# Gate building with one 256-column fp32r product a token, its high half copied by ScalarE and its low half added by VectorE

## The reference, cut to what matters

```python
s1, i1 = lax.top_k(s[:, :, 0], PEER_TOPK)
s2, i2 = lax.top_k(s[:, :, 1], PEER_TOPK)
cand = (s1[..., :, None] + s2[..., None, :]).reshape(PEER_BLOCK, PEER_HEADS, PEER_TOPK * PEER_TOPK)
sc, ic = lax.top_k(cand, PEER_TOPK)
e1 = jnp.take_along_axis(i1, ic // PEER_TOPK, axis=-1)
e2 = jnp.take_along_axis(i2, ic % PEER_TOPK, axis=-1)
idx = e1 * PEER_NKEYS + e2
gate = jax.nn.softmax(sc, axis=-1)
act = jax.nn.gelu(jnp.einsum('td,thkd->thk', xb, u[idx]).astype(jnp.float32), approximate=False)
return jnp.einsum('thk,thkd->td', (gate * act).astype(xb.dtype), v[idx])
```

## Time and profile before

| | us |
|---|---|
| median of 3 runs | 4364.64 |
| lowest and highest run | 4364.55, 4371.59 |
| the profiled execution, its own time | 4372.93 |
| the span of its trace | 4370.9 |
| mean granted TensorE clock | 0.973 |

### The profile page before, as it was taken

How to read it: one execution, slowest core, us unless ns; L and a number is a source line. 1 busy time by engine, 2 the same in 40 slices (tenths; PEclk the granted TensorE clock), 3 DMA queues, 4 the chain that set the end, 5 groups by cost and what they waited for, 6 DMA issues and landing times. The chain is left out here.

```text
span 4370.9 us, 85782 instructions
## 1 busy us (share of the span) xinstructions
PE 4123.5 (94%) x32794; PEld 3775.2 (86%) x32794; DVE 3159.1 (72%) x5937; ACT 1417.5 (32%) x2207; POOL 1317.5 (30%) x1006
## 2 busy tenths in 40 slices
PE   8999999997669979999999998999999999999998
PEld 5898888886548869787878887999999999999998
DVE  5621334444852368889976665999999999999998
ACT  4212222112552222233356774222222222222224
POOL 4333330000022200244532333444434444443441
PEclk9999999999879999999999999999999999999999
DMA  6665665564643211244435447999999999999995
GB/s 220 215 205 179 227 233 180 188 247 126 174 143 105 111 54 40 76 144 135 144 118 200 178 174 268 312 297 303 302 299 302 300 301 298 301 303 299 299 303 194
DMA packets 527665, 928.68 MB, mean 212 GB/s; under 512 B 286400, under 2 KB 353728, under 8 KB 523344
## 3 DMA queue, kind: packets, MB, share of 16 engines
q1 hardware_dynamic: 391584, 549.91, 38.5%
q0 software_dynamic: 81056, 346.96, 23.5%
q10 hardware_dynamic: 54816, 28.85, 2.3%
HBM read 786.05 MB, written 206.30 MB: 227 GB/s over the span
## 5 line engine op out<-in xcount | busy, mean ns | idle before, releaser
L3513 POOL DMA_INDIRECT ex_rows<-expert_rows,ex_here x512 | 586.7, 1146 | 953.6 <-DVE acc_tok L3734 863.8
L3734 DVE SCALAR_TENSOR_TENSOR acc_tok<-ex_rows,ex_wsp,acc_tok 128x1024 f32<-128x1024 f32 x512 | 634.5, 1281 | 0.0
L2837 PE MATMUL ex_psa<-x_dense_high,eg_u_high 128*128 128x288 f32 x2048 | 604.5, 295 | 13.4 <-ACT ex_w L3625 10.3
L2837 PE MATMUL ex_psa<-x_dense_low,eg_u_high 128*128 128x288 f32 x2048 | 604.6, 295 | 0.0
L2837 PE MATMUL ex_psa<-x_dense_high,eg_u_low 128*128 128x288 f32 x2048 | 604.2, 295 | 0.0
L2928 POOL TENSOR_TENSOR eg_u_low<-eg_u,eg_u_high 128x1024 fp32r<-128x1024 f32 x130 | 340.8, 2622 | 797.4 <-ACT eg_u_high L2923 797.4
L3545 PE MATMUL ex_pso<-ex_w_high,ex_v_high 128*128 128x288 f32 x2048 | 442.2, 298 | 7.6 <-DVE acc L3716 7.6
L3625 ACT ACTIVATE ex_w<-ex_psa 128x288 f32<-128x288 f32 x256 | 105.4, 412 | 1055.3 <-PE ex_psa L2837 1055.3
L3545 PE MATMUL ex_pso<-ex_w_high,ex_v_low 128*128 128x288 f32 x2048 | 440.7, 297 | 0.0
L3545 PE MATMUL ex_pso<-ex_w_low,ex_v_high 128*128 128x288 f32 x2048 | 439.3, 296 | 0.0
L3716 DVE TENSOR_TENSOR acc<-ex_pso,acc 128x576 f32<-128x576 f32 x512 | 374.7, 753 | 45.1 <-PE ex_pso L3545 45.1
(11 more groups left out here) (537 smaller groups left out, 9042.1 us busy)
## 6 DMA issues: line engine op xcount, KB each, us to landing
eg_u<-in_u SPq DMA_DIRECT2D x256, 512.0 KB, 5.1
expert_rows<-in_v SPq DMA_DIRECT2D x128, 512.0 KB, 7.2
ex_v<-in_v SPq DMA_DIRECT2D x128, 512.0 KB, 6.2
weights<-wt_stage SPq DMA_DIRECT2D x9, 4096.0 KB, 12.9
ex_g<-weights SPq DMA_DIRECT2D x128, 288.0 KB, 6.8
expert_rows<-eg_act SPq DMA_DIRECT2D x256, 128.0 KB, 1.7
proj<-in_out POOLq DMA_DIRECT2D x50, 548.5 KB, 6.3
in_w<-in_w_in SPq DMA_DIRECT2D x50, 512.0 KB, 5.1
```

The source lines that it names most:

```text
L2837: yield nc.tensor.matmul(out[:, 0:b - a], w[:, kc, :], half[:, kc, a:b], start=n == 0, stop=n == len(passes) - 1)
L3513: pool.indirect_dma_start(rows[i][:, :], None, table, index(here[par][:, t, j:j + 1]), element_offset=ROW_RUNS[t][0]).then_inc(s_row[i], 16)
L3734: v.scalar_tensor_tensor(out=acc_tok[:, t, :], in0=rows[i][:, at:at + D], scalar=wsp[:, i:i + 1], in1=acc_tok[:, t, :], op0=ALU.mult, op1= ...
```

## The change

BATCH becomes 4, so there are 16 batches in a block (144 in all), RING is 8 slots, FILL is 9, and FINISHED is worked out from FILL (after batches 2, 5, 7, 10, 13 and 15 of a block).

The gate is split once at the start into a high part, rounded to fp32r, and a low part (selT gets a fourth slice): ACT rounds, DVE subtracts, for the first 64 tokens and then for the others. one1 gets two matrices a token, side by side: the one-hot times the low part of the gate, and the one-hot times the high part. one2 stays a bare one-hot. Both are fp32r, and a token is one product with 256 columns, into 1 KB of PSUM: low gates, then high gates.

The one1 pair is made for the first 2 tokens of a batch by a DVE comparison into the high place and two ACT multiplications, and for the other 2 by one DVE scalar_tensor_tensor each (gated). ACT copies the high half of a batch from PSUM to stage (copy_high, 512 elements) and DVE adds the low half from PSUM to it in place (add_low, 512 elements). DVE does this for batch m - 2 within batch m, between gated and one2, and waits there for ACT's copy. ACT's order is: the copy for batch n, the gates for batch n + 2, then gelu and high where one is due. The iota gets a buffer of its own. SP's and POOL's programs stay as they are; the wait of SP for a block's last evacuation now ends with DVE's last addition.

The diff, cut to its core:

```diff
--- before.py
+++ after.py
@@ -2821,7 +2821,7 @@
-BATCH = 8
+BATCH = 4
...
@@ -3178,24 +3178,30 @@
     BANKS = 2
     SG_ = SPREAD_GROUPS
     FILL = SG_ * 3 * KC // NB
+    NHOT = NTB * NB
     HALF = BATCH // 2
+    LOW, HIGH = 2, 3
     with ExitStack() as ctx:
         sb = lambda n, s, dt=F32: ctx.enter_context(nc.sbuf_tensor(f"wt_{n}", s, dt))
         iota = sb("iota", [P, NK])
-        one1 = sb("one1", [P, RING, NK])
-        one2 = sb("one2", [P, RING, NK])
-        iota_i = one2[:, 0, :].bitcast(I32)
+        one1 = sb("one1", [P, RING, 2, NK], F32R)
+        one2 = sb("one2", [P, RING, NK], F32R)
+        iota_i = sb("iota_i", [P, NK], I32)[:, :]
         stages = sb("stage", [P, 2, NK, TB])
         stage = [stages[:, 1], stages[:, 0]]
-        ps = ctx.enter_context(nc.psum_tensor("wt_ps", [P, BANKS, BATCH, NK], F32))
+        ps = ctx.enter_context(nc.psum_tensor("wt_ps", [P, BANKS, BATCH, 2, NK], F32))
         early.banks(ctx, "wte")
         EACH, ERING = 2 * SG_, early.RING
         assert EACH % ERING == 0
         s_io = k.sem("wt_iota_step")
+        s_high = k.sem("wt_gates_rounded")
+        s_low = k.sem("wt_gates_split")
         s_st = k.s_weights_stored = [k.sem(f"wt_stored{i}") for i in range(2)]
 
         batches = [f"batch{n}" for n in range(NB)]
-        OH = Progress(k.sem("wt_onehots"), *batches)
+        hots = [f"hot{n}" for n in range(NB)]
+        CP = Progress(k.sem("wt_high_copied"), *batches)
+        OH = Progress(k.sem("wt_onehots"), *[s for pair in zip(hots, batches) for s in pair])
         GA = Progress(k.sem("wt_gated"), *batches)
         PE = Progress(k.sem("wt_matmul"), *batches)
         EV = Progress(k.sem("wt_evac"), *batches)
@@ -3220,9 +3226,8 @@
         late = TOPK_EARLY - 1 + early.RING
         late_group = (late, late % ERING, late // ERING)
 
-        def slots(n, lo=0, hi=BATCH):
-            at = n * BATCH % RING
-            return slice(at + lo, at + hi)
+        def ring(m):
+            return m * BATCH % RING
...
@@ -3258,26 +3263,47 @@
             def _(dve):
                 v = nc.vector
                 OH.credit(dve)
+
+                def split(n, lo, hi):
+                    dve.wait_ge(s_high, n)
+                    w = selT[:, LOW, lo:hi]
+                    v.tensor_tensor(w, w, selT[:, HIGH, lo:hi], ALU.subtract).then_inc(s_low, 1)
+
+                def onehots(out, side, lo, hi):
+                    return v.tensor_tensor(out, bc(iota[:, :].unsqueeze(1), [P, hi - lo, NK]),
+                                           bc(selT[:, side, lo:hi].unsqueeze(2), [P, hi - lo, NK]), ALU.is_equal)
+
+                def gated(out, c):
+                    v.scalar_tensor_tensor(out=out, in0=bc(iota[:, :].unsqueeze(1), [P, 2, NK]), scalar=selT[:, 0, c:c + 1],
+                                           in1=bc(selT[:, LOW:HIGH + 1, c:c + 1], [P, 2, NK]),
+                                           op0=ALU.is_equal, op1=ALU.mult)
+
+                def add_low(m):
+                    b, n = divmod(m, NB)
+                    dve.wait_ge(CP.sem, CP.now(batches[n], b))
+                    out = stage[b % 2][:, :, n * BATCH:(n + 1) * BATCH]
+                    v.tensor_tensor(out, out, ps[:, m % BANKS, :, 0, :].rearrange("p t f -> p f t"),
+                                    ALU.add).then_inc(*EV.inc(batches[n]))
+
+                split(1, 0, TB)
+                dve.wait_ge(s_low, 1)
                 dve.wait_ge(s_io, 2)
-
-                def body(b, slot, r):
-                    for n in range(NB):
-                        dve.wait_ge(PE.sem, PE.back(n, AHEAD, b))
-                        t0 = n * BATCH
-                        col = TB * b + t0
-
-                        def onehots(out, side, lo, hi):
-                            cnt = hi - lo
-                            return v.tensor_tensor(out[:, slots(n, lo, hi), :], bc(iota[:, :].unsqueeze(1), [P, cnt, NK]),
-                                                   bc(selT[:, side, col + lo:col + hi].unsqueeze(2), [P, cnt, NK]),
-                                                   ALU.is_equal)
-                        onehots(one1, 0, 0, BATCH)
-                        onehots(one2, 1, 0, HALF)
-                        for t in range(t0 + HALF, t0 + BATCH):
-                            last = v.tensor_scalar(one2[:, t % RING, :], iota[:, :], selT[:, 1, TB * b + t:TB * b + t + 1],
-                                                   selT[:, 2, TB * b + t:TB * b + t + 1], ALU.is_equal, ALU.mult)
-                        last.then_inc(*OH.inc(batches[n]))
-                in_line(body)
+                for m in range(NHOT):
+                    b, n = divmod(m, NB)
+                    if m == AHEAD:
+                        split(2, TB, TD)
+                    if m == NB:
+                        dve.wait_ge(s_low, 2)
+                    at, col = ring(m), BATCH * m
+                    dve.wait_ge(PE.sem, PE.back(n, AHEAD, b))
+                    onehots(one1[:, at:at + HALF, 1, :], 0, col, col + HALF).then_inc(*OH.inc(hots[n]))
+                    for t in range(HALF, BATCH):
+                        gated(one1[:, at + t, :, :], col + t)
+                    if m >= AHEAD:
+                        add_low(m - AHEAD)
+                    onehots(one2[:, at:at + BATCH, :], 1, col, col + BATCH).then_inc(*OH.inc(batches[n]))
+                for m in range(NHOT - AHEAD, NHOT):
+                    add_low(m)
 
             @block.tensor
             def _(pe):
@@ -3292,8 +3318,8 @@
                         pe.wait_ge(OH.sem, OH.now(batches[n], b))
                         pe.wait_ge(GA.sem, GA.now(batches[n], b))
                         pe.wait_ge(EV.sem, EV.back(n, BANKS, b))
-                        for t in range(n * BATCH, (n + 1) * BATCH):
-                            mm = nc.tensor.matmul(ps[:, n % BANKS, t % BATCH, :], one2[:, t % RING, :], one1[:, t % RING, :],
+                        for t in range(BATCH):
+                            mm = nc.tensor.matmul(ps[:, n % BANKS, t, :, :], one2[:, ring(n) + t, :], one1[:, ring(n) + t, :, :],
                                                   start=True, stop=True)
                         mm.then_inc(*PE.inc(batches[n]))
                         if b:
@@ -3306,39 +3332,45 @@
             @block.scalar
             def _(act):
                 GA.credit(act)
+                CP.credit(act)
                 EV.credit(act)
                 for i in range(2):
                     act.sem_inc(s_st[i], 16)
-                FINISHED = {2: 0, 3: 1, 4: 2, 6: 3, 7: 4}
-
-                def gate(b, n):
-                    act.wait_ge(OH.sem, OH.now(batches[n], b))
-                    for t in range(n * BATCH, n * BATCH + HALF):
-                        o_ = one2[:, t % RING, :]
-                        last = nc.scalar.activation(o_, o_, ACT.Copy, scale=selT[:, 2, TB * b + t:TB * b + t + 1])
+                FINISHED = {-(-3 * KC * (i + 1) // FILL) - 1: i for i in range(SG_)}
+
+                def rounded(lo, hi):
+                    nc.scalar.activation(selT[:, HIGH, lo:hi].bitcast(F32R), selT[:, LOW, lo:hi], ACT.Copy).then_inc(s_high, 1)
+
+                def gate(m):
+                    b, n = divmod(m, NB)
+                    act.wait_ge(OH.sem, OH.now(hots[n], b))
+                    for t in range(HALF):
+                        hot, c = one1[:, ring(m) + t, :, :], BATCH * m + t
+                        nc.scalar.activation(hot[:, 0, :], hot[:, 1, :], ACT.Copy, scale=selT[:, LOW, c:c + 1])
+                        last = nc.scalar.activation(hot[:, 1, :], hot[:, 1, :], ACT.Copy, scale=selT[:, HIGH, c:c + 1])
                     last.then_inc(*GA.inc(batches[n]))
 
+                def copy_high(b, slot, r, n):
+                    if n == 0:
+                        act.wait_ge(s_st[slot], 16 * r + 16)
+                    act.wait_ge(PE.sem, PE.now(batches[n], b))
+                    nc.scalar.activation(stage[slot][:, :, n * BATCH:(n + 1) * BATCH],
+                                         ps[:, n % BANKS, :, 1, :].rearrange("p t f -> p f t"),
+                                         ACT.Copy).then_inc(*CP.inc(batches[n]))
+
                 def body(b, slot, r):
-                    def evac(n):
-                        if n == 0:
-                            act.wait_ge(s_st[slot], 16 * r + 16)
-                        act.wait_ge(PE.sem, PE.now(batches[n], b))
-                        dst = stage[slot][:, :, n * BATCH:(n + 1) * BATCH].rearrange("p f t -> p t f")
-                        nc.scalar.activation(dst, ps[:, n % BANKS, :, :], ACT.Copy).then_inc(*EV.inc(batches[n]))
-
                     for n in range(NB):
-                        if n:
-                            gate(b, n)
-                            evac(n - 1)
+                        copy_high(b, slot, r, n)
+                        if NB * b + n + AHEAD < NHOT:
+                            gate(NB * b + n + AHEAD)
                         if n in FINISHED:
```

(15 more changed lines are left out.)

## The result

The changed kernel takes 4413.65 us (median of 4 runs, 4406.89 to 4417.9) against 4368.11 (4 runs, 4364.55 to 4374.26): a ratio of 1.0103, 95% interval 1.0090 to 1.0117, slower by 45.5 us. The prediction was 4413.0, range 4335 to 4465, slower with a chance of 0.64. One more run of the kernel before stands beside the three known at the prediction, and lifts its median from 4364.64 to 4368.11.

A forecast was written before the change was run, and what follows sets the result against it. PE bounds the kernel before, DVE after: 333 us of DVE steps, 95 of stalls, 56 of u waits, 1 and 5.5 make a 490.5 us stage against 442.1, +48, so 4413 us, range 4335 to 4465.

The forecast's parts named there:

- The bound: In the phase_spread stage, PE bounds the kernel before (DVE waits 162.6 us for it); after the change DVE does.
- PE's part: PE's products in the stage: 2.51 us per new batch, giving back 61 us, a 381 us stage if PE stayed the bound.
- DVE's part: DVE's steps in each of 144 new batches: 2.31 us a batch, 333 us in all.
- Rival 4: DVE's low addition reads PSUM in 1 KB steps, taking 1.01 us instead of 0.60: 37 us more, 4450 us; chance 0.14.
- The stalls: DVE instructions with two SBUF operands stand while POOL makes u low halves: 1.76 us for each of 54 operations, 95 us.
- The u waits: At 8 block ends ACT waits 7.0 us for the u tile queued behind the weights, with nothing covering it: 56 us.
- The sum: Stage total: 333 + 95 + 56 + 1 + 5.5 = 490.5 us against 442.1, +48, forecasting 4413 us.
- small edits: Roundings and splits of the gates on ACT and DVE: 1 us; iota buffer and selT slice cost nothing.
- The clock: PE's lower clock level after standing idle in the stage: no cost, at most 8 us.

The follow-up runs named there:

- e3: Changed kernel with the u load issued before the 4 MB weights store and POOL making one eighth of the stage's u low halves: 4309.90 us, ratio 0.9871.
- e4: Kernel before the change, with SP issuing a block's first u load ahead of the previous block's weights store: 4358.75 us, ratio 0.9981.
- e1: Changed kernel with SP issuing a block's first u load ahead of the previous block's 4 MB weights store: 4355.65 us, ratio 0.9974.
- e10: e1's kernel with DVE's addition of the low half moved behind one2: 4350.28 us, ratio 0.9966.
- e5: Kernel before the change, with POOL making only one eighth of each u tile's low half in the stage: 4370.01 us, ratio 0.9998.
- e2: Changed kernel with POOL making only one eighth of each u tile's low half in the stage: 4367.41 us, ratio 0.9998.
- e8: e1's kernel with ACT multiplying gates into three tokens and DVE into one in every second batch: 4371.06 us, ratio 1.0001.
- e9: e7b's kernel with ACT multiplying gates into three tokens and DVE into one in every second batch: 4368.57 us, ratio 0.9996.
- e7b: e1's kernel with DVE instead of POOL making the u low half in the stage: 4345.13 us, ratio 0.9940.
- e11: e7b's kernel with DVE's addition of the low half moved behind one2: 4333.20 us, ratio 0.9926.

## Why the prediction was right, step by step

**The bound.** It turned from PE to DVE, as predicted: 162.6 us of DVE waiting for PE became 6.5.

**PE's part.** Forecast 2.51 us a batch and a stage of 381; e3 showed 2.57 in the batch above (2.54 in the median of its batches) and 382.1. The four new products take 0.47 us, 0.12 each. Where nothing else holds the stage it is 442.1 - 382.1 = 60.0 us shorter, close to the forecast 61. Not all of that is the new product's: e3 also has the load order, which gave the kernel before 8.6 us (e4). Against e4's 433.5 the change gives back 51.4.

**DVE's part.** Forecast 2.31 us a batch; an undisturbed one runs from comparison to comparison in 2.33 (in e1's timeline from 2389.50 to 2391.83, one2 to one2). The addition of 512 elements, which was the open price, goes from start to start in 0.59 us (e10, 2392.44 to 2393.03) where 0.60 was taken. Rival 4 (1.01) is out. The prediction read "SBUF — State Buffer", section "Door 1: The DMA port swizzle", in the Trainium skill so that reading PSUM in 1 KB steps would be dear for DVE and ACT. What the Trainium skill says of PSUM there, it says of matmuls. DVE shows 678 ns an instruction and ACT 579 for the copy with the same steps, no more than contiguous reads of this size in the earlier trace rows: for these two engines the measurement decides against that reading. The other half of what it took from that section, that short runs on the SBUF side are cheap, agrees with ACT: 512 elements start to start in 0.48 us (2399.90 to 2400.38), where the old evacuation, stepping by 64 floats, took about 1 us for as many.

**The stalls.** Forecast 1.76 us for each of 54 POOL operations, 95 us; measured 77.9 us for the 53 of the stage, 1.47 each. The term was 17 us too high. The picture behind it was incomplete: I had POOL start whenever ACT released it, and in e10 it waits for the addition. That the stalls cost nothing before is shown by e5 (0.9998), and that taking them away gives 46 us now by e2; it gives no more because PE's bound is then reached.

**The u waits.** Forecast 7.0 us for each of eight, 56 us; measured 55.5 in ACT's waits and 61.5 by e1. The 15.7 us from gelu to tile came again as 15.0 (2383.95, where the gelu before the weights ends, to 2398.94), and the 8.7 after which ACT asks for it as 8.6.

**The sum.** DVE's time in the stage can be taken apart step by step, start to start: the steps as they last when undisturbed (the medians 0.335, 0.396, 0.598 and 0.602 us of its four kinds, 0.468 for the comparison of three tokens in e8 and e9, 1.135 for the u low half), what they last longer beside a POOL operation, how late the addition comes for want of ACT's copy, how late the next comparison comes for want of PE, and the two ends of the stage with the small edits. These are not printed by a view of the profile but added up from the starts in the trace.

| us | steps | stalls | addition late | waits for PE | ends | stage |
|---|---|---|---|---|---|---|
| forecast | 333 | 95 | 56 | 0 | 6.5 | 490.5 |
| changed kernel | 334.5 | 77.9 | 67.2 | 7.1 | 4.5 | 491.2 |
| e1 | 334.5 | 73.4 | 17.4 | 0 | 4.4 | 429.7 |
| e10 | 334.5 | 85.6 | 2.3 | 0 | 3.9 | 426.3 |
| e7b | 393.5 | 2.2 | 20.4 | 0 | 4.3 | 420.4 |
| e11 | 393.5 | 2.2 | 9.3 | 0 | 3.8 | 408.8 |
| e8 | 315.6 | 65.8 | 58.6 | 0 | 4.6 | 444.6 |
| e9 | 374.6 | 2.2 | 61.1 | 0 | 4.2 | 442.1 |

The mechanism of the forecast is there term by term, but that its sum came within 0.7 us is luck. The stalls were 17 us too high. Against that, the addition was late by 11 us more than the forecast 56, since it also waits for ACT's copy where no tile is late (17.4 us in e1), and the waits for PE (7.1) stood at nothing. The full time has its luck too: the change cost 45.5 us and not 48, while the median of before rose by 3.5. Going from the changed kernel to e1, the 61.5 us are 49.8 of lateness, 7.1 of waits for PE and 4.5 of stalls. The third token (e8 against e1, e9 against e7b) took off the 18.9 us of steps that it promised, and brought 41.2 and 40.7 of lateness.

**The clock.** I had this at no cost, at most 8 us, with PE having air. The window from 2400.6 to 2407.4 in the changed kernel is at the lower of the clock's two levels, 1.2 instead of 2.4 GHz (granted 0.50); it began while PE stood idle in the u wait (the columns are those of the earlier trace rows):

```profile
2400.60:2407.40 6.80, 4.38 (x12) 3.66 (x13) 6.80 (x12) 5.02 (x16) 1.82 (x1) 0.50 0.00 0
```

```profile
2407.66 0.63 PE L3322 MATMUL wt_ps<-wt_one 128*128 128x256 f32 x4
...
2408.33 0.43 DVE L3273 TENSOR_TENSOR wt_one<-wt_iota,selT 128x256 fp32r<-128x256 f32 x1 [0.71 <-PE wt_ps L3322]
```

Four products take 1.22 us instead of 0.64, and PE's first batch behind the wait takes 4.64 us (2403.02 to 2407.66) instead of 2.57. So DVE, two batches ahead, has to wait for PE: 6.5 us in eight waits, exactly one behind each of the eight u waits, the only waits for PE in the stage. Such stretches of low clock come to 72 us in the changed kernel. In e1 there is none behind the stage's first 4.2 us, and no wait of DVE for PE. No run changes the clock alone, so that the low clock causes these waits is read from the timeline; their 7 us are in the 61.5 that e1 gained. PE's busy time of 45 us in a block, where some 40 were forecast, has its slower batches in it too.

## What to carry to other kernels

When an edit makes the bounding engine cheaper by pushing work to another, add up the other engine's list together with everything that its slack was hiding: here some 50 us of stalls (what DVE waited longer in e5) and 45.5 us of waiting for tiles were already in the trace of before, and cost nothing (e5) and 9 us (e4) until PE was no longer last. Before giving an engine more work because its busy share is low, look at when its result is asked for: ACT was busy for 82% in e8, and yet the one more token on it cost more than it saved. And the cheapest repair was neither arithmetic nor layout, but one load issued ahead of a 4 MB store.

## What the runs showed of the hardware that was not expected

- While DVE issues instructions with two SBUF operands back to back, POOL can be kept out for longer than one of them: in e10 it started 0.22 us before the boundary from the gated pair to one2, did not get in there, and got in behind one2. Of 52 such operations the median lasted 3.16 us, the shortest 2.39. The Trainium skill ("SBUF — State Buffer", section "SBUF: two separate sides") has the lock pass for whole instructions to whoever starts first, and the stall that POOL itself suffers here agrees with an exclusive lock. It does not tell who wins at a boundary. In the changed kernel POOL did get in between the two gated instructions five times, each behind a u wait: DVE's pair from 2299.83, for one, then took 3.03 us instead of 0.87, with POOL's operation from 2299.93 taking 2.65. Three more times it came in while DVE waited for PE. Which boundary lets it in stays open.
- DVE's tensor_tensor of 1024 elements with both operands in SBUF lasts 1219 ns (1.14 us from its start to the next) where POOL needs 2.36 to 2.39 us, and POOL's stall on DVE was 1.37 to 1.60 us: the work is cheaper on the bounding engine than beside it (e7b, 9.3 us of stage).
